# Output projection: the right half of its columns in two quarters, and norm rows spread from channel columns

## What is computed

```python
h = layer_norm(DN_ALPHA * h + merged @ w_out[l], ln1_g[l], ln1_b[l])
ffn = group_moe(h, w_router, router_bias, w_gate_e[l], w_up_e[l], w_down_e[l])
h = layer_norm(DN_ALPHA * h + ffn, ln2_g[l], ln2_b[l])
```

## Time and profile before

| | |
|---|---|
| median of 3 runs | 781.57 us (780.5 to 782.05) |
| the profiled execution, its own time | 780.76 us |
| its span, first to last instruction | 778.7 us |
| PE busy | 740.8 us (95%) |
| DVE, ACT, POOL busy | 43%, 33%, 4% |
| moved by DMA | 251.41 MB, mean 323 GB/s |
| mean granted clock of PE | 0.991 |

### The profile page before, as it was taken

One profiled execution on the slowest core, in us unless ns is written; L12 is line 12 of the kernel. 1 busy time (PEld: TensorE's weight loads), 2 busy tenths in 40 slices (PEclk: granted clock), 3 DMA queues, 4 the chain that ended last, 5 costly groups with the idle time before them and its releaser, 6 DMA issues.

```text
span 778.7 us, 12250 instructions
## 1 busy us (share of the span) xinstructions
PE 740.8 (95%) x4334; PEld 450.5 (58%) x4335; DVE 335.4 (43%) x783; ACT 253.5 (33%) x537; POOL 29.0 (4%) x59
## 2 busy tenths in 40 slices
PE   6999999999999999999999999999999898898894
PEld 5978789998889999743333333333333332333341
DVE  6687566545768777574212221222212212202205
ACT  5675535546767555421111101111111101111111
POOL 3032000000001000000000000000000000000000
PEclk9999999999999999999999999999999999999998
DMA  9795313335040866999999999999999999999994
GB/s 278 310 348 216 144 74 138 137 157 217 2 187 30 324 274 239 390 367 385 425 426 425 425 425 431 428 423 429 429 423 431 428 423 431 429 421 433 426 421 167
DMA packets 38530, 251.41 MB, mean 323 GB/s; under 512 B 6129, under 2 KB 13394, under 8 KB 24162
## 3 DMA queue, kind: packets, MB, share of 16 engines
q1 hardware_dynamic: 38352, 250.94, 78.9%
q10 hardware_dynamic: 146, 0.04, 0.0%
HBM read 249.92 MB, written 1.05 MB: 322 GB/s over the span
## 4 chain that ended last, share of the span: by engine, by line
PE 72%; SPq 14%; DMA 6%; DVE 4%; issue 1%; ACT 1%; ACTq 0%; DVEq 0%
PE ps L2194 28%; PE ps L1798 8%; PE ps L1800 8%; PE ps L1799 8%; DMA gate_x<-in_w_gate_e_dram 6%; SPq L583 3%; PE ps L2144 3%; SPq L602 2%; SPq L572 2%; PE ps L1875 2%; PE ps L2151 2%; PE ps L2132 2%; SPq L586 2%; DVE xc L1204 1%; DVE wlo L1190 1%
## 5 line engine op out<-in xcount | busy, mean ns | idle before, releaser
L2194 PE MATMUL ps<-raw,xg 128*64 128x512 f32 x512 | 117.0, 607 | 9.0 <-DMA raw<-in_w_gate_e_dram 5.9
L1798 PE MATMUL ps<-hi_h,whi 128*128 128x272 f32 (+1 forms) x384 | 111.6, 291 | 0.4 <-DVE wlo L1121 0.3
L1800 PE MATMUL ps<-hi_h,wlo 128*128 128x272 f32 (+1 forms) x384 | 109.3, 285 | 0.0
L1799 PE MATMUL ps<-lo_h,whi 128*128 128x272 f32 (+1 forms) x384 | 109.0, 284 | 0.0
L1121 DVE TENSOR_TENSOR wlo<-raw,whi 128x512 fp32r<-128x512 f32 x128 | 82.6, 687 | 38.6 <-ACT whi L751 38.0
L2194 PEld LDWEIGHTS ps<-raw,xg 128*64 128x64 f32 x512 | 38.0, 140 | 85.2 <-issue 75.8
L751 ACT CAST whi<-raw 128x512 fp32r<-128x512 f32 (+1 forms) x128 | 74.1, 619 | 14.6 <-PE ps L1800 12.3
L1798 PEld LDWEIGHTS ps<-hi_h,whi 128*128 128x128 f32 x384 | 72.3, 188 | 4.3 <-issue 2.5
L1800 PEld LDWEIGHTS ps<-hi_h,wlo 128*128 128x128 f32 x384 | 72.4, 188 | 0.0
L1799 PEld LDWEIGHTS ps<-lo_h,whi 128*128 128x128 f32 x384 | 72.3, 188 | 0.0
L2194 PE MATMUL ps<-gate_x,xg 128*64 128x512 f32 x256 | 57.1, 594 | 7.7 <-DMA gate_x<-in_w_gate_e_dram 7.7
(11 more groups left out here) (367 smaller groups left out, 1152.6 us busy)
## 6 DMA issues: line engine op xcount, KB each, us to landing
raw<-in_w_up_e_dram SPq DMA_DIRECT2D x16, 2048.0 KB, 34.1
gate_x<-in_w_gate_e_dram SPq DMA_DIRECT2D x16, 2048.0 KB, 37.1
raw<-in_w_down_e_dram SPq DMA_DIRECT2D x16, 2048.0 KB, 34.3
raw<-in_w_gate_e_dram SPq DMA_DIRECT2D x15, 2048.0 KB, 36.4
raw<-in_w_in_dram SPq DMA_DIRECT2D x28, 1024.0 KB, 9.1
down_x<-in_w_down_e_dram SPq DMA_DIRECT2D x8, 2048.0 KB, 38.0
up_x_right<-in_w_up_e_dram SPq DMA_DIRECT2D x16, 1024.0 KB, 38.8
up_x_left<-in_w_up_e_dram SPq DMA_DIRECT2D x8, 2048.0 KB, 37.7
```

The source lines that it names most:

```text
L1798: mm(o, w1, hi[:, k, c0:c0 + n], start=(k == 0), stop=False)
L1799: mm(o, w1, lo[:, k, c0:c0 + n], start=False, stop=False)
L1800: last = mm(o, w2, hi[:, k, c0:c0 + n], start=False, stop=(k == KB - 1))
L2194: last = mm(ps[r0:r0 + SLOTS, bank_no, :], lhs[:, k % 4, k // 4, :], w[:, k % 2, 512 * c:512 * c + 512], start=(k == 0), stop=(k == KB - 1))
```

## The change

The right half of `w_out`'s columns becomes two quarters of 256 columns. Pieces 8 to 11 belong to the first quarter, 12 to 15 to the second; each of them holds two row blocks. DVE's residual and statistics, and PE's turns, are done for each part; both turns of the right half stand before the router products, and five fillers go. The table load on ACT moves ahead of the copies. `diag`, `row_sel`, their 16 DMAs and POOL's memsets go; instead PE clears each bank with a bfloat16 matmul of 512 columns whose weights are zero, and adds four float32 matmuls of 128 columns that spread a column of `chan` by the identity. `down_y[1]` is issued right behind `gate_x`. The last two fillers ahead of the first expert go too.

```diff
+        if section == "out" and half:
+            quarter, pair = divmod(k, 4)
+            c0 = 512 + 256 * quarter
+            return raw[:, slot_of(section), 2 * pair:2 * pair + 2, c0:c0 + 256]
...
+    OUT_PART = ((0, 512), (512, 256), (768, 256))
...
+                sp.dma_start(flat(down_y[1][:]), flat(four_rows(w_down[0, 1], 1)[:, 2:4, :])).then_inc(down_y_in[1], 16)
             sp.wait_ge(s.lo_ready, PIECES * done)
...
-                sp.wait_ge(s.diag_zero, 2)
-                for r0, v in ((0, ln1_g), (32, ln1_b)):
-                    for k in range(KB):
-                        sp.dma_start(diag[r0 + k:r0 + k + 1, P * k:P * k + P], v[0:1, P * k:P * k + P]).then_inc(s.diag_in, 16)
...
-        sp.wait_ge(s.rows_b, 2)
-        sp.dma_start(flat(down_y[1][:]), flat(four_rows(w_down[0, 1], 1)[:, 2:4, :])).then_inc(down_y_in[1], 16)
...
-        pool.memset(diag[:], 0.0).then_inc(s.diag_zero, 1)
...
+        act.activation(table_load[:], neglam[0:1, :], ACT.Exp)
         for b in range(4):
-            if b == 2:
-
-                act.activation(table_load[:], neglam[0:1, :], ACT.Exp)
...
+        for part, used in ((1, 12), (2, PIECES)):
+            dve.wait_ge(s.pieces_used, OUT_BASE + used + NBUF)
+            for t in range(TT):
+                residual_part(t, part)
+            for t in range(TT):
+                stats_part(t, part)
...
+            for i, k in enumerate(ks):
+                w1, w2 = (w[:, n % NBUF, width_n * i:width_n * i + width_n] for w in (whi, wlo))
+                for t in range(TT):
+                    o = out_bank(part, t)
+                    c = slice(P * t, P * t + P)
+                    mm(o, mg_hi[:, k, c], w1, start=(k == 0), stop=False)
+                    mm(o, mg_lo[:, k, c], w1, start=False, stop=False)
+                    last = mm(o, mg_hi[:, k, c], w2, start=False, stop=(k == KB - 1))
             last.then_inc(s.pieces_used, 1)
             if n == PIECES - 2:
...
-                turn_half(0)
+                turn_part(0)
+        turn_part(1)
+        turn_part(2)
         logits(0)
-        keep_warm(4, 2)
-        turn_half(1)
-        keep_warm(4, 3)
         logits(1).then_inc(s.ht_t1, 1)
...
+        def clear(bank_no, alone):
+
+            mm(ps[:, bank_no, :].rearrange("p (r c) -> p r c", c=P), zero_b[:].to_broadcast([P, P]),
+               before_b[:].unsqueeze(1).to_broadcast([P, 4, P]), start=True, stop=alone, skip_group_check=True)
+
+        def spread(column, c, bank_no):
+
+            clear(bank_no, False)
+            for k in range(4 * c, 4 * c + 4):
+                last = mm(ps[:, bank_no, P * (k % 4):P * (k % 4) + P], chan[:, column + k:column + k + 1].to_broadcast([P, P]),
+                          ident[:], start=False, stop=True, skip_group_check=True)
+            return last
 
         for c in range(2):
-            spread(1, c, B_ACC[c])
-        spread(0, 0, 2)
+            spread(C_L1B, c, B_ACC[c])
+            clear(B_ACC[2 + c], True)
+        spread(C_L1G, 0, 2)
         pe.wait_ge(s.router_exp, 1)
-        spread(0, 1, 1).then_inc(s.rows_b, 2)
+        spread(C_L1G, 1, 1).then_inc(s.rows_b, 2)
         keep_warm(0, 3)
...
-        keep_warm(0, 2)
         def unit(u, e, odd):
```

More of the change, by code:

```diff
@@ L141, in build @@
     minus_half = perm("minus_half", [P, 2 * AH])
-    row_sel = perm("row_sel", [P, 2])
+    zero_b = perm("zero_b", [P, 1], BF16)
     group_sum = perm("group_sum", [P, NE])
@@ L241, in build @@
     rt = at("rt", [P, 16, TT * NE], split_area - work)
-    diag = at("diag", [P, D], F + 24576)
     xsb = at("xsb", [P, 512], F + 2048)
@@ L454, in half_row, with ring_row, out_bank @@
         half, k = divmod(n, KB)
+        if section == "out" and half:
+            quarter, pair = divmod(k, 4)
+            c0 = 512 + 256 * quarter
+            return raw[:, slot_of(section), 2 * pair:2 * pair + 2, c0:c0 + 256]
         return raw[:, slot_of(section), k, 512 * half:512 * half + 512]
+    def ring_row(buf, section, n):
+        if section == "out" and n >= KB:
+            return buf[:, n % NBUF, :].rearrange("p (a c) -> p a c", c=256)
+        return buf[:, n % NBUF, :]
+    OUT_PART = ((0, 512), (512, 256), (768, 256))
+    def out_bank(part, t):
+        return ps[:, 4 + 2 * t + part % 2, 0:OUT_PART[part][1]]
     FIRST_PIECE = {OG: PIECES * OG, "out": OUT_BASE}
@@ L634, in _ @@
         own = Steps(pool, s.pool)
-        for t, v in ((ident, 0.0), (late, 0.0), (ahead, 0.0), (before, 1.0), (one, 1.0), (one_b, 1.0), (first, 0.0), (ve, 1.0), (mparts, 0.0),
+        for t, v in ((ident, 0.0), (late, 0.0), (ahead, 0.0), (before, 1.0), (one, 1.0), (one_b, 1.0), (zero_b, 0.0), (first, 0.0), (ve, 1.0), (mparts, 0.0),
                      (minus_half, -0.5)):
@@ L808, in split_half_row @@
             act.wait_ge(s.pieces_used, FIRST_PIECE[section] + n + 1)
-            act.copy(whi[:, n % NBUF, :], half_row(section, n)).then_inc(s.hi_ready, 1)
+            act.copy(ring_row(whi, section, n), half_row(section, n)).then_inc(s.hi_ready, 1)
         def conv_first(blk, odd):
@@ L1189, in split_half_row @@
             dve.wait_ge(s.hi_ready, FIRST_PIECE[section] + n + 1)
-            dve.tensor_tensor(wlo[:, n % NBUF, :], half_row(section, n), whi[:, n % NBUF, :].bitcast(F32),
+            dve.tensor_tensor(ring_row(wlo, section, n), half_row(section, n), ring_row(whi, section, n).bitcast(F32),
                               ALU.subtract).then_inc(s.lo_ready, 1)
@@ L1512, in _, with residual_part, stats_part @@
         merged_lo(KB, 0)
[L1513 to L1520, removed]
+        def residual_part(t, part):
+            c0, n = OUT_PART[part]
+            dve.scalar_tensor_tensor(out=h1[:, t, c0:c0 + n], in0=hres[:, t, c0:c0 + n], scalar=ALPHA, in1=out_bank(part, t),
+                                     op0=ALU.mult, op1=ALU.add).then_inc(s.resid_done, 1)
+        def stats_part(t, part):
+            c0, n = OUT_PART[part]
+            dve.wait_ge(s.resid_done, TT * part + t + 1)
+            for q in range(c0 // 256, (c0 + n) // 256):
+                own(dve.bn_stats(stats8[:, 4 * t + q, :], h1[:, t, 256 * q:256 * q + 256]))
         dve.wait_ge(s.hres_ready, TT)
@@ L1526, in _ @@
                 dve.wait_ge(s.pieces_used, OUT_BASE + KB + NBUF)
-                residual_half(0, 0)
+                residual_part(0, 0)
             elif n == KB + NBUF:
-                residual_half(1, 0)
+                residual_part(1, 0)
             elif n in (KB + NBUF + 1, KB + NBUF + 2):
[L1531 to L1536, removed]
+                stats_part(n - (KB + NBUF + 1), 0)
+        for part, used in ((1, 12), (2, PIECES)):
[4 more added lines that the diff above has]
+                stats_part(t, part)
         own.settle()
         for t in range(TT):
-            own(dve.bn_aggr(mv[:, t, :], stats[:, t, :, :]))
+            own(dve.bn_aggr(mv[:, t, :], stats8[:, 4 * t:4 * t + 4, :]))
         own.settle()
@@ L1708, in add_base @@
                 dve.wait_ge(s.base_made, 2 * (1 - t) + c + 1)
-                dve.tensor_tensor(ps[:, B_ACC[2 * t + c], :], ps[:, B_ACC[c], :], staged[c][:],
-                                  ALU.add).then_inc(s.acc_base, 1)
+                dve.scalar_tensor_tensor(out=ps[:, B_ACC[2 * t + c], :], in0=ps[:, B_ACC[c], :], scalar=ALPHA,
+                                         in1=staged[c][:], op0=ALU.mult, op1=ALU.add).then_inc(s.acc_base, 1)
         scaled_norm(1)
@@ L2052, in _, with turn_part @@
         stream(WA, ya_hi, ya_lo, 0, (evac[GB], KB + 2))
-        def turn_half(half):
+        def turn_part(part):
+            c0, n = OUT_PART[part]
             for t in range(TT):
-                pe.wait_ge(s.resid_done, TT * half + t + 1)
-                for k in range(4 * half, 4 * half + 4):
+                pe.wait_ge(s.resid_done, TT * part + t + 1)
+                for k in range(c0 // P, (c0 + n) // P):
                     last = pe.transpose(turned1[:, k, P * t:P * t + P], h1[:, t, P * k:P * k + P], ident[:])
@@ L2072, in _ @@
         for n in range(PIECES):
-            half, k = divmod(n, KB)
-            if half == 0:
-                pe.wait_ge(s.mg_lo_s, k + 1)
-            pe.wait_ge(s.lo_ready, OUT_BASE + n + 1)
[L2077 to L2082, removed]
+            if n < KB:
+                part, ks = 0, (n,)
+                pe.wait_ge(s.mg_lo_s, n + 1)
+            else:
+                part, pair = 1 + (n - KB) // 4, n % 4
+                ks = (2 * pair, 2 * pair + 1)
+                if n == KB + 4:
+                    pe.wait_ge(s.resid_done, TT)
+            width_n = OUT_PART[part][1]
+            pe.wait_ge(s.lo_ready, OUT_BASE + n + 1)
+            for i, k in enumerate(ks):
[6 more added lines that the diff above has]
+                    last = mm(o, mg_hi[:, k, c], w2, start=False, stop=(k == KB - 1))
             last.then_inc(s.pieces_used, 1)
```

13 lines of the change are left out of this document (removed).

## The result

| | before | after |
|---|---|---|
| median of 16 runs each, one chip | 780.48 us (779.98 to 782.05) | 782.82 us (781.53 to 784.29) |
| ratio, 95% interval | | 1.0025 (1.0019 to 1.0032) |
| the profiled execution, its own time | 780.76 us | 783.46 us |
| its span | 778.7 us | 781.4 us |
| mean granted clock of PE | 0.991 | 0.991 |

By the ratio the change costs 0.25%, 2.0 us (1.5 to 2.5), where +1.05 was forecast; the two medians are 2.3 us apart.

A forecast was written before the change was run, and what follows sets the result against it. PE's and DVE's path from "out" to expert 0's up product, which releases expert 2's up transfer, was taken as the bound. -0.42 and +1.51, rounded to +1.06, gave +1.05 us on 781.57: 782.6 us, range 779.4 to 784.4.

The forecast's parts named there:

- Pieces of 256: In "out" on PE, 48 matmuls of 512 columns become 96 of 256, so the last piece ends 0.65 us later.
- Less work behind the last piece: Between the last piece of "out" and the logits, less residual, turn and copy work remains: -0.42 us.
- The norm rows: On PE ahead of the ranks, 22 small and clearing matmuls take 4.94 us instead of 3.43: +1.51 us.
- The fillers: Without the two ahead of the first expert, the gate product starts 0.6 us sooner relative to the gather; up still decides.
- The up release decides: Expert 0's up product frees the buffer for expert 2's up, 1.4 us later than the gate release counting bytes.
- The moved megabyte: `down_y[1]` behind `gate_x` fills the gap at 322 with 2.46 us of transfer; it buys nothing by itself.
- Its span plus 2.1: The profiled execution of the kernel before, 780.76 us, taken as first to last instruction plus 2.1 us.
- theory C: From the experiments: the loss's rest, about 1 us, comes from outside this stage, from the program's start or by chance.
- Dearer spread: Rival: the 22 norm-row matmuls take 7.2 us, ranks come at +3.3, time 784.9 us; chance 0.11.
- Transfers set the restart: Rival: expert 2's bytes stand behind the first two experts' queue, the end comes 2.2 us sooner, 779.4; chance 0.17.
- Rows cost no more: Rival: the norm rows cost no more than before, so -0.42 stands alone, 781.2 us; chance 0.09.
- The clock: Rival: PE's clock falls since seven fillers are gone; one fall adds 1.7 us, 784.3; chance 0.03.

The follow-up runs named there:

- e1: The changed kernel run again with no edit, beside the kernel before; ratio to the kernel before 1.0017.
- e4: The changed kernel with only the 1 MiB of `down_y[1]` issued late, at the end of the dense stage; ratio to the kernel before 1.0020.
- e7: The changed kernel with the two fillers ahead of the first expert put back; ratio to the kernel before 1.0022.
- e2: The kernel before with the new norm rows, `diag` gone and `down_y[1]` behind `gate_x`; halves and fillers as before; ratio to the kernel before 1.0018.
- e5: The changed kernel with the last norm-row spread moved behind the rank matmuls and the three fillers ahead of the ranks removed; ratio to the kernel before 1.0003.
- e8: The changed kernel with all 22 matmuls of the norm rows done twice; ratio to the kernel before 1.0069.
- e6: e5 with DVE reading bank 1's gain row for both tiles first, so the up product waits for two `scaled_norm`, not four; ratio to the kernel before 0.9992.
- e11: The kernel before with only DVE's order changed, bank 1 of both tiles first, so the up product waits for two `scaled_norm`; ratio to the kernel before 0.9998.
- e12: e6 run again, without a further edit; ratio to the kernel before 0.9981.
- e10: The kernel before with nothing but POOL's memset of `zero_b` added; ratio to the kernel before 0.9995.

## Why the path was right and the sum too small, point by point

The time lay in the range (782.8 in 779.4 to 784.4), and the sign and the path were right. The likeliest case was a loss within 0.2% of before. The loss came out at that bound: 1.0025 (from 1.0019) in the first comparison, 1.0017, 1.0020 and 1.0022 in e1, e4 and e7.

- **Pieces of 256.** +0.65 forecast, +0.73 measured, of which 0.08 is one matmul behind the turn of the left half (328.68 to 328.88, 0.20 where 0.12 is usual). The Trainium skill ("TensorE: Matmul & The Clock Gate", section "Back-to-back issue gap") gives 109 and 216 ns, by which it would have been +0.1; it gives them for the isolated matmul, and about 131 ns at 512 columns for a sustained stream, where the float32r rows here show 226. The measured pitch decided rightly. The clearing matmul's step of 0.22 agrees with the Trainium skill's isolated 216 ns.
- **Less work behind the last piece.** -0.42 forecast, -0.44 measured. The two residuals took 0.75 (0.76 forecast). The "about 0.2" for the first of the last two transposes stood on no row; residual to ACT's copy took 0.54 in after (331.68 less 331.14) and 0.56 in the forecast.
- **The norm rows.** +1.51 forecast, +1.43 measured (e2), 0.08 of it the 22 matmuls coming out at 4.86 and not 4.94. That they are on the path was right: e2, e5 and e8.
- **The fillers.** Here a term was mis-sized: 0.6 was taken, 0.34 measured (e7). The step let the product start when PE's register reads end, at 343.97 + 0.90 = 344.87 in after, and overlooked that `xg` comes as late, at 344.89, and the product 0.27 behind it. It did not reach the time, as forecast.
- **The up release decides.** Right: lag less up is 413.6 to 414.3 in all 14 profiles, while the up product moves over 7.4 us. e6, e11 and e12 move it without the gate product, and the lag moves with it.
- **The moved megabyte.** Worth nothing, as forecast (e4). It fills the hole at 322 and lengthens that at 346, before the same release of PE.
- **The sum, "taken whole by the up release: +1.05".** The path gave +0.93, and it arrives. e1, e4 and e7 have the same path, and their spans are 0.49, 0.95 and 1.30 us over before's, 0.91 in the mean. A straight line through the twelve spans of the table gives 0.95 us of span for 1 us of up, and -0.03 for an unmoved up product. The times of the three are 1.3 to 1.7 us over before's (ratio times 781.4), because something else came on top.
- **"Its span plus 2.1."** Here the sum was short. The 2.1 us over the span were carried over from before to after without a term for them. Measured are 2.5 to 2.7 in the mean of each of the seven kernels that are built like after, so about 0.5 us more, outside of everything the forecast worked out. This answers theory C: the rest of the loss comes from outside the stage, but from the end of the program and not from its start (e10). The first comparison has some 0.7 us beyond that. Before's times are low in it, 780.7 in the mean against 780.9 to 781.5 in the others; whether that is chance stays open.
- **The class.** +1.05 was put at 0.13% against a bound of 0.2%, with 0.47 of 0.60 inside it. With the 0.5 of the last point the middle would have stood at the bound of 1.6 us. The forecast had no term for what two programs differ by beside the path, nor did its share beyond the bound allow for one.
- **The rivals.** Dearer spread: no, 4.86. Transfers set the restart: no (e4, and 0 GB/s at 346). Rows cost no more: no (e2). The clock: the granted clock is 1.00 in every window read from 320 to 375, and e7's fillers change nothing.

## What to carry to other kernels

In this kernel the queue of transfers stands empty until an engine frees a buffer. There only the release that comes last in the sense of bytes (its time less the transfer time of what stands ahead of it) was worth shortening; sending something sooner into that queue only made it empty for longer. In another kernel, look for such a hole first. Before adding matmuls to an engine's program, look for the place where it waits for another engine anyway: the same norm row cost 1.1 us ahead of the ranks and 0.2 behind them. And where a consumer waits for a count, ask which of the counted steps it needs: waiting for two of four, in the right order, took 1.36 us off the up product. Last, where a difference of 1 us matters, compare spans beside times: here half a us of the loss lay behind the last instruction.

## What the runs showed that was not expected

- DVE's two additions into the banks take 1.50 us in e6, where the second also waits for a semaphore, and 1.29 in after. It costs nothing here, PE no longer waiting for them.
- The queue does not come back at once: after the restart it moves 387 GB/s in 350 to 358 us and 389 in 358 to 370 (after), 378 and 388 (before, each in its own frame), against 427 in the steady stage, in both kernels alike:

```profile
350.00:358.00 8.00, 6.93 (x34) 2.55 (x32) 6.67 (x12) 1.18 (x2) 0.00 (x0) 1.00 1.01 387
358.00:370.00 12.00, 12.00 (x64) 5.19 (x62) 3.96 (x11) 0.59 (x1) 0.00 (x0) 1.00 0.97 389
```
